# Cross-attention output and first gate tile by row blocks, with the gate's features split straight from PSUM

## The chip, the cores and the metric

One Trainium2 chip, one core. The metric is the device time of one execution in microseconds, lower is better; a kernel's time is the median of its runs.

## The reference

Two transformer blocks on 256 rows of width 2048, all in float32. The change lies in the second block, between the output projection of its cross attention and the gate of its feed-forward part:

```python
y = memory_cross_attention(h, mem_n, w_xq, w_xkv, w_xo)   # its last step: (256 x 512) @ w_xo (512 x 2048)
x = x + rms_norm_2(y, ln_x_post)                          # norm over each row's 2048 values
h = rms_norm_2(x, ln_ffn_pre)
y = (silu(h @ w_gate) * (h @ w_up)) @ w_down              # D_FF 5632
x = x + rms_norm_2(y, ln_ffn_post)
```

## The kernel before

**Products.** A weight matrix streams in as chunks of 512 rows by 512 columns (1 MB); half a chunk, 256 rows, is a *half*. The Scalar engine rounds a half into `whi` (`hi`, a 128x1024 cast, the helper's line 596) and the Vector engine puts the rest, raw minus `whi`, into `wlo` (`lo`, line 1415). Features stand transposed in `xhi` and `xlo` (128 features x 256 rows, 16 blocks `kb`), split in the same way. `half(q, ...)` on TensorE makes 12 matmuls of 512 columns: for two blocks of features and both row blocks b (rows 0 to 127 and 128 to 255), xhi by whi, xhi by wlo, xlo by whi (lines 2454 to 2456). It waits for `lo_done`, and its last matmul raises `pe_half`. `whi` and `wlo` hold four halves, so `hi(q)` waits until half q-4 has been used. A tile of 512 output columns takes two PSUM banks, one for each row block; `free(t)` makes TensorE wait until the tile two back has been read (`evicted`).

**The stretch of the change.** The output projection xo has four tiles of two halves each (q = xo0 to xo7), and TensorE goes through them tile by tile. After each tile the Scalar engine takes the sums of squares of both row blocks (`post_squares`, line 642) and the Vector engine multiplies the tile by the norm's gain into `ybuf` (`post_gained`, line 1591). After the last tile `post_norm(1)` works out 1/rms (lines 1609 to 1612), and `post_rows` (line 1600) adds `ybuf` times 1/rms to the residual h, 512 columns of one row block at a time. Then `turn_group` transposes h on TensorE in quads: four 128x128 transposes of one row block, one PSUM bank each, two quads a group (line 2520). The Vector engine multiplies a quad by the gain into `stage_t` (`turned_rows`, line 1527), the Scalar engine rounds it into `xhi` (`hi_group`, line 596), and the Vector engine writes the rest to `xlo` (`lo_group`, line 1538).

**The order.** Each engine works through one list written out by hand, and the engines meet at semaphores; nothing is planned at run time. TensorE: xo0 to xo7; group 0; then the gate's halves f0 to f7 over both row blocks, with groups 1, 2 and 3 behind f0, f2 and f4. Half f0 waits for the split of group 0, f2 for group 1, f4 for group 2 and f6 for group 3. Half f8, the first of the up projection, comes next. On the Scalar engine `square_sums(6)` (two passes over h, line 705) and a square root stand between the last `hi_group` and `hi` of f8; the Vector engine's `row_scale(6)` (lines 1505 and 1507) belongs to it. The DMA queue (SyncE) loads a chunk when `lo` of the chunk four back is done.

Of the kernel before, what the change touches and what calls it, by code (L numbers as in the profile page):

```python
# [3217 lines left out]
```

## Time and profile before

| | |
|---|---|
| median of 3 runs | 2511.58 us (2508.11 to 2513.05) |
| profiled execution | 2507.73 us, its span 2505.9 us |
| TensorE busy | 2474.0 us, 99% of the span |
| Vector engine busy | 1552.3 us, 62% |
| Scalar engine busy | 1238.7 us, 49% |
| mean granted TensorE clock | 0.997 |

Times in rows are microseconds from the start of the span unless marked ns. In the profile DVE is the Vector engine, ACT the Scalar engine, PE TensorE's matmuls and PEld its weight loads. A matmul's duration overlaps the next one's, so the pitch of the starts tells what it costs. The profiled execution is 1.83 us longer than its span and 3.85 us under the median.

### The profile page before, as it was taken

To read this page: it belongs to the slowest core of one execution; us is meant where nothing else is said; L and a number is where in the kernel's file an instruction comes from. 1 tells how busy PE (TensorE), PEld (TensorE's weight loads), DVE (VectorE), ACT (ScalarE), POOL (GpSimd) and SP (SyncE) were. 2 spreads that over 40 slices of the span, in tenths; PEclk is the share of its full clock that TensorE was granted. 3 is DMA by queue.
4 is the path that set the end of the run, shared out by engine and by line. 5 is a ranking of instruction groups with operands and counts; after the bars stand their busy time and mean duration, and the time that the engine had idled before them with its cause. 6 is when DMAs were issued, how large, how long until landed. Compare 5 with 4: busy or idle time off the path is not lost.

```text
span 2505.9 us, 31485 instructions
## 1 busy us (share of the span) xinstructions
PE 2474.0 (99%) x12033; PEld 2157.0 (86%) x12033; DVE 1552.3 (62%) x1941; ACT 1238.7 (49%) x1622; POOL 70.2 (3%) x57
## 2 busy tenths in 40 slices
PE   9999999999999999999999999999899999999998
PEld 8888888888888888888888778888788888888887
DVE  7576475655565655676555666766755555555557
ACT  7475554544444545445443445565554444444444
POOL 1022120000000000000000000000000000000000
PEclk9999999999999999999999999999999999999999
DMA  9655656656566565656654446675466666666664
GB/s 356 187 160 164 207 191 195 196 186 207 195 201 201 192 210 185 210 191 224 213 168 135 154 140 196 230 245 185 134 215 199 200 198 198 198 200 200 200 201 135
DMA packets 244712, 488.77 MB, mean 195 GB/s; under 512 B 11984, under 2 KB 13296, under 8 KB 243856
## 3 DMA queue, kind: packets, MB, share of 16 engines
q1 hardware_dynamic: 240592, 470.35, 58.0%
q0 software_dynamic: 3312, 13.92, 1.5%
q10 hardware_dynamic: 720, 3.29, 0.4%
q8 instruction: 60, 0.98, 0.2%
q14 instruction: 28, 0.23, 0.0%
HBM read 485.43 MB, written 2.10 MB: 195 GB/s over the span
## 4 chain that ended last, share of the span: by engine, by line
PE 95%; DVE 3%; ACT 2%; issue 1%; DMA 0%; DVEq 0%; ACTq 0%; SPq 0%
PE ps_a L2454 24%; PE ps_a L2456 24%; PE ps_a L2455 24%; PE ps_b L2454 5%; PE ps_b L2455 5%; PE ps_b L2456 5%; PE ps_b L2797 1%; DVE wlo L1415 1%; PE ps_b L2520 1%; PE ps_b L2585 0%; PE ps_b L2871 0%; ACT whi L596 0%; PE ps_b L2861 0%; ACT prob L1087 0%; PE ps_b L2886 0%
## 5 line engine op out<-in xcount | busy, mean ns | idle before, releaser
L1415 DVE TENSOR_TENSOR wlo<-raw,whi 128x1024 fp32r<-128x1024 f32 x872 | 1069.4, 1236 | 681.8 <-ACT whi L596 680.0
L596 ACT CAST whi<-raw 128x1024 fp32r<-128x1024 f32 x880 | 911.1, 1045 | 965.8 <-PE ps_a L2456 743.0
L2454 PE MATMUL ps_a<-whi,xhi 128*128 128x512 f32 x1888 | 725.5, 384 | 8.9 <-DVE wlo L1415 5.9
L2455 PE MATMUL ps_a<-wlo,xhi 128*128 128x512 f32 x1888 | 717.0, 380 | 0.0
L2456 PE MATMUL ps_a<-whi,xlo 128*128 128x512 f32 x1888 | 716.9, 380 | 0.0
L2454 PEld LDWEIGHTS ps_a<-whi,xhi 128*128 128x128 f32 x1888 | 357.8, 190 | 65.3 <-issue 11.0
L2456 PEld LDWEIGHTS ps_a<-whi,xlo 128*128 128x128 f32 x1888 | 357.7, 189 | 50.8
L2455 PEld LDWEIGHTS ps_a<-wlo,xhi 128*128 128x128 f32 x1888 | 357.9, 190 | 48.6
L2454 PE MATMUL ps_a<-whi,x2hi 128*128 128x512 f32 x640 | 244.8, 383 | 1.1 <-DVE wlo L1415 1.1
L2456 PE MATMUL ps_a<-whi,x2lo 128*128 128x512 f32 x640 | 242.7, 379 | 0.0
L2455 PE MATMUL ps_a<-wlo,x2hi 128*128 128x512 f32 x640 | 242.7, 379 | 0.0
L2454 PEld LDWEIGHTS ps_a<-whi,x2hi 128*128 128x128 f32 x640 | 121.1, 189 | 18.5 <-DVE wlo L1415 1.1
L2456 PEld LDWEIGHTS ps_a<-whi,x2lo 128*128 128x128 f32 x640 | 121.1, 189 | 17.1
L2455 PEld LDWEIGHTS ps_a<-wlo,x2hi 128*128 128x128 f32 x640 | 121.1, 189 | 16.4
L2454 PE MATMUL ps_b<-whi,uhi 128*128 128x512 f32 x320 | 121.4, 379 | 0.0
L2455 PE MATMUL ps_b<-wlo,uhi 128*128 128x512 f32 x320 | 121.3, 379 | 0.0
L2456 PE MATMUL ps_b<-whi,ulo 128*128 128x512 f32 x320 | 121.3, 379 | 0.0
L2454 PE MATMUL ps_a<-whi,muhi 128*128 128x512 f32 x272 | 103.4, 380 | 0.0
L2455 PE MATMUL ps_a<-wlo,muhi 128*128 128x512 f32 x272 | 103.1, 379 | 0.0
L2456 PE MATMUL ps_a<-whi,mulo 128*128 128x512 f32 x272 | 103.1, 379 | 0.0
L2455 PE MATMUL ps_b<-wlo,muhi 128*128 128x512 f32 x240 | 91.0, 379 | 0.0
L2456 PE MATMUL ps_b<-whi,mulo 128*128 128x512 f32 x240 | 91.0, 379 | 0.0
(406 smaller groups left out, 2217.3 us busy)
## 6 DMA issues: line engine op xcount, KB each, us to landing
raw<-in_w_in SPq DMA_DIRECT2D x108, 1024.0 KB, 5.6
raw<-in_w_up SPq DMA_DIRECT2D x108, 1024.0 KB, 5.4
raw<-in_w_down SPq DMA_DIRECT2D x108, 1024.0 KB, 5.0
raw<-in_w_gate SPq DMA_DIRECT2D x44, 1024.0 KB, 5.1
raw<-in_w_out SPq DMA_DIRECT2D x16, 1024.0 KB, 5.1
raw<-in_w_mix_out SPq DMA_DIRECT2D x16, 1024.0 KB, 6.3
raw<-in_w_br_attn SPq DMA_DIRECT2D x8, 1024.0 KB, 5.1
raw<-in_w_br_pool SPq DMA_DIRECT2D x8, 1024.0 KB, 5.0
```

Source lines behind the costliest of these rows:

```text
L596: return nc.scalar.copy(o, i)
L1415: return V.tensor_tensor(wlo[:, q % 4], raw[:, c % SLOTS, 2 * j:2 * j + 2], whi[:, q % 4].bitcast(F32), ALU.subtract).then_inc(lo_done, 1)
L2454: mm(o, x0, m0, start=first and j == 0, stop=False)
L2455: mm(o, x0, m1, start=False, stop=False)
L2456: ins = mm(o, x1, m0, start=False, stop=last and j == len(kbs) - 1)
L2520: ins = nc.tensor.transpose(o[:, m * P:(m + 1) * P], src[:, b, (kb + m) * P:(kb + m + 1) * P], ident)
L2797: ins = nc.tensor.transpose(ps[:, (b * 4 + j) * P:(b * 4 + j + 1) * P], src[:, b, j * P:(j + 1) * P], ident)
```

## The change

The semaphores `last_half` and `last_added`, used at the end of the kernel, are renamed `row_tile` and `row_taken` and counted on from what the new stretch adds; two counts of `post_std` and `post_var` at the end go up by one. The rest of the change is this:

- Tiles 2 and 3 of xo run by row blocks (`half_rows`, six matmuls): both tiles for b = 0, then both for b = 1. Only the b = 1 pass raises `pe_half`. Tiles 0 and 1 stay as they were.
- Squares, gain and norm of tiles 2 and 3 are taken per row block; each row block has its own norm and root.
- f0 to f3 run for b = 0, then for b = 1; f4 to f7 over both.
- Transposes come one quad at a time in the order `ROW_QUADS` (row block, column tile), eight turns instead of four groups.
- `turned_rows` and `stage_t` go: `row_hi` (Scalar) and `row_lo` (Vector) read the quad in PSUM, four instructions of 128x128 each with the gain as their per-partition scale.

```diff
...
+ROW_QUADS = ((0, 0), (0, 1), (1, 0), (1, 1), (0, 2), (1, 2), (0, 3), (1, 3))
+def row_quad(k):
+    b, j = ROW_QUADS[k]
+    bank_ = bank(4 + (QUADS["n6"][0] + k + 2) % 4)
+    return [(4 * j + m, slice(b * P, (b + 1) * P), bank_[:, m * P:(m + 1) * P]) for m in range(4)]
...
-    rest_xo = linear("xo", 0, 4, lambda t, tile, q: post_squares(tile, q), kchunks=1, opened=2, late=2)
-    c0, q0, _ = seg["ffn"]
-    for k in range(2):
-        hi(q0 + k, chunk=c0 + k // 2)
-    rest_xo()
-    post_norm(1)
-    for j in range(4):
-        if j == 0:
-            act.wait_ge(pe_half, q_end("xo"))
-        hi_group("n6", j, xhi)
-        if j < 3:
-            for k in range(2 * j + 2, 2 * j + 4):
-                hi(q0 + k, chunk=c0 + k // 2)
+    some("xo", 2, 4)
+    _, qx_, tx = seg["xo"]
+    post_squares(tx, qx_ + 2)
+    some("xo", 4, 8)
+    post_squares(tx + 1, qx_ + 4)
+    def row_squares_of(b, t):
+        if b:
+            act.wait_ge(pe_half, qx_ + 2 * t + 2)
+        else:
+            act.wait_ge(row_tile, t - 1)
+        act.wait_ge(post_sq, 8 + 4 + 2 * b + t - 2)
+        nc.scalar.activation(junk2[:, b * NT:(b + 1) * NT], bank(2 * (t % 2) + b), ACT.Square,
+                             accum_out=s_pp[:, 4 * b + t:4 * b + t + 1]).then_inc(post_sq, 1)
+    def row_root(b):
+        act.wait_ge(post_var, 2 + b)
+        nc.scalar.activation(s_pstd[:, b:b + 1], s_pvar[:, b:b + 1], ACT.Sqrt).then_inc(post_std, 1)
+    def row_hi(k):
+        act.wait_ge(t_ps, QUADS["n6"][0] + k + 1)
+        if k == 0:
+            act.wait_ge(pe_half, qx_ + 4)
+        for kb, r, ps in row_quad(k):
+            ins = nc.scalar.activation(xhi[:, kb, r], ps, ACT.Copy, scale=gain_t[:, G_FFN + kb:G_FFN + kb + 1])
+        ins.then_inc(t_hi, 1)
+    row_squares_of(0, 2)
+    row_squares_of(0, 3)
+    row_root(0)
+    some("ffn", 0, 1)
+    row_hi(0)
+    some("ffn", 1, 2)
+    row_hi(1)
+    row_squares_of(1, 2)
+    some("ffn", 2, 3)
+    row_squares_of(1, 3)
+    row_root(1)
+    some("ffn", 3, 4)
+    row_hi(2)
+    row_hi(3)
+    for k in range(4, 8):
+        some("ffn", k, k + 1)
+        row_hi(k)
     square_sums(6)
     act.wait_ge(post_done, 16)
...
     xo_gained = post_gained(1)
-    linear("xo", 0, 4, lambda t, tile: xo_gained(t, tile) if t < 3 else None, kchunks=1, opened=2, late=2)
-    c0, q0, t0 = seg["ffn"]
-    ffn_gain = gain_t[:, G_FFN:G_FFN + 16]
-    for k in range(2):
-        lo(q0 + k, chunk=c0 + k // 2)
-    post_norm(1)
-    post_group(0)
-    for j in range(4):
-        turned_rows("n6", j, ffn_gain)
-        if j == 1:
-            xo_gained(3, t0 - 1)
-        lo_group("n6", j, xhi, xlo)
-        if j < 3:
-            post_group(j + 1)
-            for k in range(2 * j + 2, 2 * j + 4):
-                lo(q0 + k, chunk=c0 + k // 2)
+    _, qx_, tx = seg["xo"]
+    def row_gained(b, t):
+        dve.wait_ge(post_sq, 8 + 4 + 2 * b + t - 1)
+        return V.tensor_tensor(streams(ybuf[:, b, t * NT:(t + 1) * NT]), columns(2 * (t % 2) + b),
+                               streams(post_gain[:, t * NT:(t + 1) * NT]), ALU.mult)
+    def row_norm(b):
+        dve.wait_ge(post_sq, 8 + 4 + 2 * b + 2)
+        link(V.reduce_sum(s_psq[:, b:b + 1], s_pp[:, 4 * b:4 * b + 4], axis=AX))
+        V.tensor_scalar(s_pvar[:, b:b + 1], s_psq[:, b:b + 1], 1.0 / D, EPS, ALU.mult, ALU.add).then_inc(post_var, 1)
+    def row_norm_end(b):
+        dve.wait_ge(post_std, 2 + b)
+        link(V.reciprocal(s_prstd[:, b:b + 1], s_pstd[:, b:b + 1]))
+    def row_residual(k):
+        b, t = ROW_QUADS[k]
+        post_rows([(t, b)])
+    def row_lo(k):
+        dve.wait_ge(t_hi, QUADS["n6"][0] + k + 1)
+        for kb, r, ps in row_quad(k):
+            ins = V.scalar_tensor_tensor(xlo[:, kb, r], ps, gain_t[:, G_FFN + kb:G_FFN + kb + 1], xhi[:, kb, r].bitcast(F32),
+                                         ALU.mult, ALU.subtract)
+        ins.then_inc(t_lo, 1)
+    some("xo", 2, 4)
+    dve.wait_ge(pe_half, qx_ + 2)
+    xo_gained(0, tx)
+    some("xo", 4, 8)
+    dve.wait_ge(pe_half, qx_ + 4)
+    xo_gained(1, tx + 1)
+    row_gained(0, 2).then_inc(row_taken, 1)
+    row_norm(0)
+    row_norm_end(0)
+    row_residual(0)
+    row_residual(1)
+    some("ffn", 0, 1)
+    row_lo(0)
+    some("ffn", 1, 2)
+    row_lo(1)
+    link(row_gained(0, 3))
+    some("ffn", 2, 3)
+    row_norm(1)
+    row_norm_end(1)
+    row_residual(2)
+    some("ffn", 3, 4)
+    row_gained(1, 2).then_inc(evicted, 1)
+    row_lo(2)
+    row_residual(3)
+    row_lo(3)
+    row_gained(1, 3).then_inc(evicted, 1)
+    dve.wait_ge(evicted, tx + 4)
+    for k in range(4, 8):
+        row_residual(k)
+        some("ffn", k, k + 1)
+        row_lo(k)
     row_scale(6)
     c0, q0, _ = seg["ffn"]
...
-    for t in range(1, 4):
-        tile("xo", t, 1)
-    def residual_added(j):
-        pe.wait_ge(post_done, 8 + 2 * (j + 1))
+    tile("xo", 1, 1)
+    def half_rows(q, b, o, k, first, last):
+        pe.wait_ge(lo_done, q + 1)
+        w0, w1_ = whi[:, q % 4], wlo[:, q % 4]
+        for j, kb in enumerate((2 * k, 2 * k + 1)):
+            x0, x1 = xhi[:, kb, b * P:(b + 1) * P], xlo[:, kb, b * P:(b + 1) * P]
+            m0, m1 = walked(w0[:, j]), walked(w1_[:, j])
+            mm(o, x0, m0, start=first and j == 0, stop=False)
+            mm(o, x0, m1, start=False, stop=False)
+            ins = mm(o, x1, m0, start=False, stop=last and j == 1)
+        if b:
+            ins.then_inc(pe_half, 1)
+        return ins
+    def row_turn(k):
+        n = QUADS["n6"][0] + k
+        b, j = ROW_QUADS[k]
+        pe.wait_ge(post_done, 8 + k + 1)
+        if k < 4:
+            pe.wait_ge(t_y, n - 3)
+        else:
+            pe.wait_ge(t_lo, n - 3)
+        for kb, _, ps in row_quad(k):
+            ins = nc.tensor.transpose(ps, h[:, b, kb * P:(kb + 1) * P], ident)
+        ins.then_inc(t_ps, 1)
+    free(t0 + 2)
+    for t in (2, 3):
+        if t == 3:
+            free(t0 + 3)
+        for k in range(2):
+            ins = half_rows(q0 + 2 * t + k, 0, bank(2 * (t % 2)), k, k == 0, k == 1)
+        ins.then_inc(row_tile, 1)
+    for t in (2, 3):
+        for k in range(2):
+            half_rows(q0 + 2 * t + k, 1, bank(2 * (t % 2) + 1), k, k == 0, k == 1)
+            if (t, k) in ((2, 1), (3, 0)):
+                row_turn(t - 2)
+    def split_rows(k):
+        pe.wait_ge(t_lo, QUADS["n6"][0] + k + 1)
     c0, q0, tile0 = seg["ffn"]
-    turn_group("n6", h, residual_added, 0)
-    for k in range(8):
-        if k == 0:
+    pe.wait_ge(row_taken, 1)
+    for b in range(SB):
+        if b:
             pe.wait_ge(evicted, tile0 - 1)
+        for k in range(4):
+            if k % 2 == 0:
+                split_rows(2 * b + k // 2)
+            half_rows(q0 + k, b, bank(b), k, k == 0, False)
+            if k % 2:
+                row_turn(2 + 2 * b + k // 2)
+    for k in range(4, 8):
         if k % 2 == 0:
-            pe.wait_ge(t_lo, QUADS["n6"][0] + k + 2)
-        half(q0 + k, (0, 1), (2 * k, 2 * k + 1), k == 0, k == 7)
-        if k in (0, 2, 4):
-            turn_group("n6", h, residual_added, k // 2 + 1)
+            split_rows(k + 1)
+        half(q0 + k, (0, 1), (2 * k, 2 * k + 1), False, k == 7)
+        if k < 6:
+            row_turn(k + 2)
     pe.wait_ge(evicted, tile0)
```

## Rows read from the trace of the kernel before

**Rows 1.** Busy time of each engine over the whole span, the page's first part.
```profile
PE 2474.0 (99%) x12033; PEld 2157.0 (86%) x12033; DVE 1552.3 (62%) x1941; ACT 1238.7 (49%) x1622; POOL 70.2 (3%) x57
```
**Rows 2.** TensorE's waits: for whom, us in total, times, longest.
```profile
PE ps_b L2520 <- DVE h L1600: 3.6, 1, 3.6
PE ps_a L2454 <- issue: 2.2, 1, 2.2
```
**Rows 3.** Timeline of TensorE from xo7 to f8: start, us, idle before.
```profile
1789.88 0.38 PE L2456 MATMUL ps_a<-whi,xlo 128*128 128x512 f32 x1
1793.90 1.77 PE L2520 MATMUL ps_b<-base,h 128*128 128x128 f32 x8 [3.64 <-DVE h L1600]
1797.88 0.77 PE L2454 MATMUL ps_a<-whi,xhi 128*128 128x512 f32 x1 [2.21 <-issue]
...
1802.07 1.04 PE L2520 MATMUL ps_b<-base,h 128*128 128x128 f32 x8
1802.86 0.46 PE L2454 MATMUL ps_a<-whi,xhi 128*128 128x512 f32 x1
1803.16 0.38 PE L2455 MATMUL ps_a<-wlo,xhi 128*128 128x512 f32 x1
...
1825.15 0.45 PE L2454 MATMUL ps_a<-whi,xhi 128*128 128x512 f32 x1 [0.90 <-DVE wlo L1415]
```
**Rows 4.** Timeline of the Scalar engine, the same stretch and what leads to it.
```profile
1779.93 0.60 ACT L642 ACTIVATE junk<-ps_a 128x512 f32<-128x512 f32 x1 [2.02 <-PE ps_a L2456]
1781.09 2.00 ACT L596 CAST whi<-raw 128x1024 fp32r<-128x1024 f32 x2
1790.30 0.60 ACT L642 ACTIVATE junk<-ps_a 128x512 f32<-128x512 f32 x1 [2.02 <-PE ps_a L2456]
1817.93 1.91 ACT L705 ACTIVATE junk<-h 128x2048 f32<-128x2048 f32 x1
```
**Rows 5.** Timeline of the Vector engine, the same stretch.
```profile
1780.76 1.29 DVE L1591 TENSOR_TENSOR ybuf<-ps_a,post_gain 128x512 f32<-128x512 f32 x2 [1.41 <-ACT junk L642]
1782.17 2.36 DVE L1415 TENSOR_TENSOR wlo<-raw,whi 128x1024 fp32r<-128x1024 f32 x2
1791.59 0.16 DVE L1609 TENSOR_REDUCE small<-small 128x2 f32<-128x8 f32 x1 [1.89 <-ACT junk L642]
1792.43 1.41 DVE L1600 SCALAR_TENSOR_TENSOR h<-ybuf,small,h 128x512 f32<-128x512 f32 x2
1802.71 1.29 DVE L1527 TENSOR_TENSOR stage_t<-ps_b,gains 128x512 f32<-128x512 f32 x2 [1.34 <-PE ps_b L2520]
```
**Rows 6.** The nearest small pieces, Scalar engine: four of 128x128 from PSUM with a per-partition scale.
```profile
136.29 1.14 ACT L900 ACTIVATE proj<-ps_a,small 128x128 f32<-128x128 f32 x4
137.30 1.06 ACT L596 CAST whi<-raw 128x1024 fp32r<-128x1024 f32 x1
```
**Rows 7.** The nearest small pieces, Vector engine; the last row groups 128x128 reads of PSUM.
```profile
344.91 1.66 DVE L1769 SCALAR_TENSOR_TENSOR olo_a<-ps_b,gains,ohi 128x256 fp32r<-128x256 f32 x4 [1.79 <-ACT ohi L991]
L1769 DVE SCALAR_TENSOR_TENSOR olo_a<-ps_b,gains,ohi 128x256 fp32r<-128x256 f32 x8 | 3.3, 477 | 1.8 <-ACT ohi L991 1.8
L2061 DVE CUSTOM_DVE_ANT_0 prob<-ps_b,bias 128x128 f32<-128x128 f32 x32 | 9.1, 284 | 0.0
```
**Rows 8.** Stretches: us, PE busy, PEld, DVE, ACT, POOL, PEclk, DMA share, GB/s.
```profile
1757.70:1762.30 4.60, 2.33 (x19) 1.95 (x18) 4.40 (x11) 3.50 (x6) 0.00 (x0) 1.00 0.00 0
1793.90:1797.88 3.98, 1.77 (x9) 1.40 (x9) 2.77 (x5) 2.06 (x3) 0.00 (x0) 0.53 0.07 27
1797.88:1801.00 3.12, 3.12 (x8) 2.50 (x9) 3.12 (x4) 1.07 (x2) 0.00 (x0) 0.50 0.00 0
1801.00:1825.15 24.15, 22.51 (x114) 18.90 (x113) 17.94 (x27) 14.27 (x18) 0.00 (x0) 1.00 0.48 158
```
**Rows 9.** Timeline of TensorE ahead of the 16 transposes of the attention weights.
```profile
1757.70 0.38 PE L2456 MATMUL ps_a<-whi,x2lo 128*128 128x512 f32 x1
1760.35 1.97 PE L3050 MATMUL ps_b<-base,pr 128*128 128x128 f32 x16 [2.27 <-DVE pr L2304]
```

More of the change, by code:

```diff
@@ L306, in hybrid_blocks_kernel @@
         u_row_done, u_tps, u_hi, u_lo, d_add = sem("u_row"), sem("u_tps"), sem("u_hi"), sem("u_lo"), sem("down_added")
-        last_half, last_add = sem("last_half"), sem("last_added")
+        row_tile, row_taken = sem("row_tile"), sem("row_taken")
         ns = {n: sem("nsa_" + n) for n in ("dup", "tk", "xpe", "zero", "t2", "t2s", "hid", "gelu", "hidt", "hidr", "kv", "kvs", "t1", "t1s",
@@ L1295, in _ @@
                     n = 4 * b + t
-                    act.wait_ge(last_add, n + 1)
+                    act.wait_ge(row_taken, 1 + n + 1)
                     if n > 1:
@@ L1300, in _ @@
                                          accum_out=s_pp[:, n:n + 1]).then_inc(post_sq, 1)
-                act.wait_ge(post_var, 3 + b)
+                act.wait_ge(post_var, 4 + b)
                 nc.scalar.activation(s_pstd[:, b:b + 1], s_pvar[:, b:b + 1], ACT.Sqrt).then_inc(post_std, 1)
@@ L2382, in last_sum @@
             def last_sum(b, t):
-                dve.wait_ge(last_half, 4 * b + t + 1)
+                dve.wait_ge(row_tile, 2 + 4 * b + t + 1)
                 d = streams(ybuf[:, b, t * NT:(t + 1) * NT])
-                V.tensor_tensor(d, d, columns((2, 3, 0, 1)[t] if b == 0 else 4 + t), ALU.add).then_inc(last_add, 1)
+                V.tensor_tensor(d, d, columns((2, 3, 0, 1)[t] if b == 0 else 4 + t), ALU.add).then_inc(row_taken, 1)
             def last_gain(b, t):
-                dve.wait_ge(last_add, 4 * b + t + 1)
+                dve.wait_ge(row_taken, 1 + 4 * b + t + 1)
                 c = slice(t * NT, (t + 1) * NT)
@@ L2398, in last_rows @@
                 V.tensor_scalar(s_pvar[:, b:b + 1], s_psq[:, b:b + 1], 1.0 / D, EPS, ALU.mult, ALU.add).then_inc(post_var, 1)
-                dve.wait_ge(post_std, 3 + b)
+                dve.wait_ge(post_std, 4 + b)
                 link(V.reciprocal(s_prstd[:, b:b + 1], s_pstd[:, b:b + 1]))
@@ L3089, in _ @@
                 half(q0 + k, (2 * (t0 % 2), 2 * (t0 % 2) + 1), (2 * k, 2 * k + 1), k == 0, k == 1)
-            for t in range(1, 4):
-                tile("xo", t, 1)
-            def residual_added(j):
-                pe.wait_ge(post_done, 8 + 2 * (j + 1))
-            assert seg["xo"][2] % 2 == 0
+            tile("xo", 1, 1)
[11 more added lines that the diff above has]
+                return ins
@@ new lines, in row_turn @@
+            def row_turn(k):
[9 more added lines that the diff above has]
+                ins.then_inc(t_ps, 1)
+            assert t0 % 2 == 0
@@ L3165, in _ @@
                             ins = mm(o, x1, m0, start=False, stop=kb == 3)
-                    ins.then_inc(last_half, 1)
+                    ins.then_inc(row_tile, 1)
 _INS = ["x", "mem", "w_in", "gla_a_w2", "fox_f_b", "w_mem_kv", "w_out", "w_up", "w_down", "mem_2", "ln_mix_post_2", "ln_x_post_2",
```

## The prediction

> **What bounds the kernel now.** The page's busy times come first: TensorE is busy for 2474.0 of 2505.9 us, the Vector engine for 62% [rows 1]. Only what fills a hole of TensorE, or opens one, moves the time. Its waits come next, and two of the longest single ones belong to the stretch of the change: 3.6 us for the residual h, and 2.2 us before the first gate matmul, marked "issue" [rows 2]. The timeline gives their place [rows 3]: the last matmul of xo starts at 1789.88 and the first of f0 at 1797.88, with eight transposes between. The squares of tile 1 start at 1779.93 and those of tile 3 at 1790.30 [rows 4], so two tiles (48 matmuls) take 10.37 us, 0.216 us each. So xo ends at 1790.10, f0 starts 7.78 us later, and tile 1 ended at 1779.74. In the hole the clock falls to the lower level: granted 0.53 from 1793.90 and 0.50 to 1801.00, then 1.00 [rows 8]. f0, twelve matmuls that should take 2.59 us, lasts from 1797.88 to 1802.07, 1.60 us too long.
>
> From 1779.74 to the start of f8 at 1825.15 [rows 3] pass 45.41 us. Tiles 2 and 3 and f0 to f7 are 144 matmuls, 31.07 us. The other 14.34 us are holes, slow clock and transposes: that is all the change can touch. Behind f8 the same loop goes on as before, so the change is worth what it does to the start of f8.
>
> **What stays, and the prices.** Matmuls, transposes (32), weights and their DMAs keep their number. A 512-column residual add costs 0.66 us behind another and 0.75 alone, a gain 0.60 and 0.69, `lo` 1.14 and 1.22 [rows 5], `hi` 0.95 and 1.05 [rows 4]; squares with their accumulator read take 0.58 (1779.93 to 1781.09 for two [rows 4]), 0.70 until readable. A norm takes 0.84 from its sum to the first residual add (1791.59 to 1792.43 [rows 5]). Four transposes take 0.40 (eight in 0.79 [rows 3]), the matmul behind a switch or a stall 0.08 more (pitch 0.30 at 1802.86 [rows 3]). A quad can be read 0.64 after its turn starts (1802.07 to 1802.71 [rows 3, 5]), 0.70 after a stall. Between engines I take 0.04 to 0.08.
>
> **The new split.** `row_hi` is four 128x128 reads of PSUM with a per-partition scale. The nearest row has just that form: four in 1.14, the next instruction 1.01 after the first [rows 6]. `row_lo` has no row. Four reads of PSUM of 256 columns in the same operation take 1.66 at 0.477 each, a pitch of 0.39 [rows 7]; 512 columns have a pitch of 0.66 [rows 5]; that is 0.27 for 256 columns, so 0.26 for a piece of 128 and 1.13 for four. From the start of a turn to the matmul that uses the quad it is then 0.70 + 0.04 + 1.13 + 0.04 + 1.13 + 0.08 = 3.1 us. Bounds: no less than one 512-column instruction each (0.60 on the Scalar engine, like the read of 1779.93 [rows 4], 0.69 on the Vector engine, like that of 1802.71 [rows 5]), and no more than four whole durations without overlap, 4 x 0.38 and 4 x 0.34 (0.477 less 0.13; 0.284 is the shortest 128-column read of PSUM [rows 7]).
>
> The Trainium skill ("VectorE: DVE Perf Modes", section on the errata of SBUF-source operations) says that an instruction pays a fixed cost whatever its size, and advises pieces of 512 elements or more, which speaks against four pieces of 128. By its figures for reads of PSUM a piece would take an estimated 0.25 us on the Scalar engine and 0.26 on the Vector engine; the sum by it would be the same, and the row of the Scalar engine (0.253) agrees.
>
> **The walk along the three queues**, in times of the old span:
> 1. Tile 2 for b = 0 ends at 1782.33. Tile 3 needs the banks of tile 1, whose gain used to run from 1780.76 to 1782.05 [rows 5], long before tile 3. Now `hi` of xo7 stands ahead of the squares (1779.90 to 1780.95, it waits for the end of tile 1), and `lo` of xo7 ahead of the gain (to 1782.13). The two gains end at 1783.42 and TensorE has stood for 1.17.
> 2. Tile 3 for b = 0 ends at 1786.18, its squares at 1787.08, the residual add of quad 0 at 1788.76. Meanwhile tile 2 for b = 1 runs until 1788.77. Turn 0 waits 0.07. Turn 1 and tile 3 for b = 1 run to 1792.45, and the split of quad 0 is there at 1791.82. So f0 starts at once: the hole of 7.78 and the 1.60 of slow clock are gone.
> 3. f0 and f1 for b = 0 end at 1795.04. Turn 2 needs the norm of b = 1. xo7 is done at 1792.45, but its squares stand behind `hi` f1, `row_hi` 1, the squares of tile 2 and `hi` f2 and start at 1794.01; the norm's sum stands behind `lo` f2 (to 1795.78). The residual ends at 1797.42: turn 2 at 1797.50, 2.46 lost.
> 4. Turn 3 needs a residual that stands behind `lo` f3, a gain and `row_lo` 2, which waits for `row_hi` 2: 1801.22, 0.59 lost. Turn 4 stands behind `row_lo` 3 and a gain: 1805.67, 1.32 lost. Turn 5 behind `row_lo` 4: 1809.39, 0.59 lost.
> 5. f4 wants the quad that turn 5, just ahead of it, brings: a bare split, 1812.45, 2.52 lost. Before, a half of 2.59 stood between a group and its use.
> 6. Turn 7 waits for the residual behind `row_lo` 6 (0.59), and f6 for turn 7 (2.52): 1821.85.
> 7. The squares of h start behind `row_hi` 7 at 1820.48. From their start to f8 it was 7.22 (1817.93 to 1825.15 [rows 3, 4]), now 7.19: f8 at 1827.67, 0.56 behind f7.
>
> The waits: 1.17 + 0.07 + 2.46 + 0.59 + 1.32 + 0.59 + 2.52 + 0.59 + 2.52 + 0.56 = 12.39. With 31.07 for matmuls, 8 turns of 0.48 (3.84) and 0.63 for ten restarts it is 47.93, against 45.41: **2.5 us slower**. The same walk along the old lists puts f8 at 1825.11; it stands at 1825.15.
>
> The loads are hidden: the chunk of f6 and f7 is asked for when `lo` of xo7 ends (1782.13; before, at 1784.53 [rows 5]) and is wanted at 1811; that of f8 behind `lo` f1 at 1792.9, wanted at 1825, and the queues were busy for 0.48 of this stretch or less [rows 8]. GpSimd has nothing here. The later end-of-kernel edits are names and counts: nothing.
>
> The profiled execution becomes 2507.73 + 2.5 = 2510.2. The median shown is 3.85 above that execution; 2511.58 + 2.5 = **2514.1 us**. With the cheap bounds for the pieces the walk gives 2.9 less than before, with the dear ones 7.0 more.
>
> **Rivals.** *The clock falls again.* Before, it fell after 3.64 us with no work [rows 3, 8]; it stayed at 1.00 through 2.27 us of nothing followed by sixteen transposes [rows 8, 9]. In the new order TensorE has only four transposes from 1808.80 to 1812.45 and from 1818.20 to 1821.85, and the longest empty piece is 2.5 us, nearer the row that kept it. If it falls ahead of f4 or f6, that half costs 1.60 more, as f0 did (f6 has the 0.56 ahead of f8 as cover): +4.1 with f4 alone, +5.2 with both, +6.8 if f2 behind turn 2 falls too. The point from which it decides is an empty piece of more than 2.3 and less than 3.6 us; with two or more the kernel is over 0.2% slower.
>
> *Pieces do not overlap on the Vector engine.* Then a `row_lo` takes 1.37 and the walk gives +4.2; with both engines so, +7.0. Against it: four pieces take 1.66, not 4 x 0.477 [rows 7].
> The Trainium skill ("VectorE: DVE Perf Modes", "The DRAIN you can't avoid") says that the next operation does not start before the pipeline has emptied. Read so, it would be this rival; the row of four pieces speaks against that reading.
>
> *Pieces are cheap*: as little as one wide instruction. f4 and f6 then wait 1.6 instead of 2.5, the other waits shrink too, and the time is up to 2.9 less.
>
> *The waits of steps 3, 5 and 6 do not come* and the removed hole is a gain: 2.5 - 2.46 - 2 x 2.52 = -5.0. For it: the hole is real and its filling certain. Against it: no size of a piece within the bounds gives it, and the order of TensorE's list puts f4 right behind turn 5.
>
> **Chances.** As walked (-0.5 to +4.5): 0.60. Cheap pieces: 0.08. Clock: 0.15, of which 0.09 for two falls or more. No overlap on the Vector engine 0.06, on both 0.05. The gain: 0.06. About 0.2%, 5.0 us, is what a measurement of this kernel can tell from no change. Faster by more than that: 0.06. Slower by more: 0.09 + 0.05 and 0.08 for the upper ends of the others and the scatter of the runs (4.9 us over three), 0.22. The rest, 0.72, is within. The range goes from -2.9 (cheap pieces) to +7.9 (dear pieces or three falls, with some scatter): 2508.7 to 2519.5.
>
> **What would show it.** Right: no hole of 7.8 us behind xo, clock at 1.00 there; a wait of 1.2 before tile 3 for the gain in `ybuf`; one of about 2.5 for h before turn 2; two of about 2.5 for `xlo` before f4 and f6; a quad's four pieces in about 1.1 us on each engine; f8 about 2.5 later after tile 1. Wrong: `xlo` waits under 1.5 (pieces cheap), a granted clock under 1 behind a turn (the clock), or f8 earlier than before.

## The result: 4.1 us slower, and where they are in the profile after

The changed kernel takes 2514.95 us in the median of 22 runs (2513.1 to 2516.81), the kernel before 2510.82 (22 runs, 2508.11 to 2513.05): the ratio is 1.0017 [1.0011, 1.0022], 2.8 to 5.5 us more. 2514.1 was predicted. The difference itself was predicted as +2.5, from a base of 2511.58, the median of three runs, which lies 0.76 above that of 22. So the time is close, in part by luck of the base, and the difference was 1.6 us short. Those 1.6 us are what there is to explain.

The profiled execution of the changed kernel takes 2515.64 us, its span is 2513.2: 7.91 more than the one before. Measured by the starts of TensorE's matmuls, 2.19 of them stand ahead of the change (tile 1 of xo ends at 1781.93 instead of 1779.74, in code that both kernels share), 0.61 outside the span, nothing behind f8 (from there to the end 680.72 and 680.75 us), and 5.14 in the stretch from the end of tile 1 to f8: 50.55 us instead of 45.41.

Most of the 2.19 us ahead of the stretch has one place. The sixteen transposes of the attention weights, which kept the full clock in the profile before [rows 8, 9], ran at the lower level here, behind a wait of the same length:

```profile
1760.88 3.63 PE L3136 MATMUL ps_b<-base,pr 128*128 128x128 f32 x16 [2.28 <-DVE pr L2344]
1764.17 0.56 PE L2540 MATMUL ps_a<-whi,x2hi 128*128 128x512 f32 x1
```

Before, the matmul behind them started at 1762.07:

```profile
1762.07 0.46 PE L2454 MATMUL ps_a<-whi,x2hi 128*128 128x512 f32 x1
```

They took 3.29 us instead of 1.72, which is 1.57 of the 2.19. The experiments come back to this place.

TensorE's waits in this stretch, in the view of waits (for whom, us in total, times, longest), answering [rows 2]:

```profile
PE ps_b L3202 <- DVE h L1640: 4.8, 5, 2.3
PE ps_a L2540 <- DVE xlo L2384: 4.8, 2, 2.4
PE ps_a L3185 <- DVE ybuf L1631: 1.1, 1, 1.1
```

The hole of [rows 3] is gone, and with it "issue". In its place stand eight waits, five of them for the residual h ahead of a turn, two for the split of one quad, one for the banks of tile 3. The timeline of TensorE tells where (start, us, instruction, idle before), and what the two longest do to the clock:

```profile
1785.74 0.48 PE L3185 MATMUL ps_a<-whi,xhi 128*128 128x512 f32 x1 [1.06 <-DVE ybuf L1631]
...
1799.52 0.66 PE L3202 MATMUL ps_b<-base,h 128*128 128x128 f32 x4 [2.27 <-DVE h L1640]
...
1811.38 0.66 PE L3202 MATMUL ps_b<-base,h 128*128 128x128 f32 x4 [0.46 <-DVE h L1640]
...
1814.42 0.48 PE L2540 MATMUL ps_a<-whi,xhi 128*128 128x512 f32 x1 [2.40 <-DVE xlo L2384]
...
1815.63 0.63 PE L2542 MATMUL ps_a<-whi,xlo 128*128 128x512 f32 x1
1816.06 0.63 PE L2540 MATMUL ps_a<-whi,xhi 128*128 128x512 f32 x1
...
1825.51 0.53 PE L2540 MATMUL ps_a<-whi,xhi 128*128 128x512 f32 x1 [2.40 <-DVE xlo L2384]
```

A turn is the four transposes of one quad. Turn 5 starts at 1811.38, f4 at 1814.42, turn 6 at 1818.62: f4 lasts 4.20 us. Inside it the pitch of the matmuls (from one start to the next) goes from 0.22 to 0.43 (1815.63 to 1816.06). The same stretches by windows (us, PE busy, PEld, DVE, ACT, POOL, PEclk, DMA share, GB/s), answering [rows 8]:

```profile
1811.38:1814.42 3.04, 0.65 (x4) 0.41 (x4) 2.25 (x6) 2.08 (x5) 0.00 (x0) 1.00 0.23 43
1814.42:1818.62 4.20, 4.20 (x13) 3.31 (x14) 1.74 (x2) 0.00 (x0) 0.00 (x0) 0.64 0.58 218
1825.51:1829.24 3.73, 3.73 (x9) 2.99 (x10) 0.34 (x2) 3.23 (x6) 0.00 (x0) 0.54 0.66 254
```

The clock is up in the hole and at its lower level (1.2 GHz) for most of f4 and of f6: granted 0.64 and 0.54.

The new split, which had no row before, on the Scalar and on the Vector engine:

```profile
1800.21 1.14 ACT L1261 ACTIVATE xhi<-ps_b,gains 128x128 fp32r<-128x128 f32 x4 [0.80 <-PE ps_b L3202]
1801.39 1.12 DVE L2384 SCALAR_TENSOR_TENSOR xlo<-ps_b,gains,xhi 128x128 fp32r<-128x128 f32 x4
1802.43 0.74 DVE L1640 SCALAR_TENSOR_TENSOR h<-ybuf,small,h 128x512 f32<-128x512 f32 x1
```

Busy times over the span, against [rows 1]: TensorE has the same 12033 matmuls, and its 5.7 us more are for the most part records stretched by the lower clock, which the two profiles have at different places.

```profile
PE 2479.7 (99%) x12033; PEld 2159.8 (86%) x12033; DVE 1551.3 (62%) x1960; ACT 1243.1 (49%) x1647; POOL 70.3 (3%) x57
```

### The profile page after: what moved, and what is told of

Its sections match the earlier page's. It is cut to its first block, busy times and chain, and to the rows that moved or that the text cites. A ratio compares the mean times of both kernels' runs of the same rounds, so it can differ in the third digit from the quotient of the medians.

```text
span 2513.2 us, 31528 instructions
## 1 busy us (share of the span) xinstructions
PE 2479.7 (99%) x12033; PEld 2159.8 (86%) x12033; DVE 1551.3 (62%) x1960; ACT 1243.1 (49%) x1647; POOL 70.3 (3%) x57
## 3 DMA queue, kind: packets, MB, share of 16 engines
q10 hardware_dynamic: 720, 3.29, 0.4%
## 4 chain that ended last, share of the span: by engine, by line
PE 95%; DVE 2%; ACT 2%; issue 1%; DVEq 0%; ACTq 0%
PE ps_a L2540 24%; PE ps_a L2541 24%; PE ps_a L2542 24%; PE ps_b L2541 5%; PE ps_b L2542 5%; PE ps_b L2540 5%; PE ps_b L2883 1%; PE ps_b L2957 1%; PE ps_b L2671 0%; DVE wlo L1455 0%; PE ps_b L2606 0%; ACT whi L604 0%; DVE xlo L2384 0%; PE ps_b L2947 0%; ACT prob L1095 0%
## 5 line engine op out<-in xcount | busy, mean ns | idle before, releaser
L2540 PE MATMUL ps_a<-whi,xhi 128*128 128x512 f32 x1856 | 713.9, 385 | 8.5 <-DVE xlo L2384 4.8
L2541 PE MATMUL ps_a<-wlo,xhi 128*128 128x512 f32 x1856 | 705.9, 380 | 0.0
L2542 PE MATMUL ps_a<-whi,xlo 128*128 128x512 f32 x1856 | 705.7, 380 | 0.0
L2540 PEld LDWEIGHTS ps_a<-whi,xhi 128*128 128x128 f32 x1856 | 352.2, 190 | 63.4 <-issue 6.9
L2542 PEld LDWEIGHTS ps_a<-whi,xlo 128*128 128x128 f32 x1856 | 352.3, 190 | 50.3
L2541 PEld LDWEIGHTS ps_a<-wlo,xhi 128*128 128x128 f32 x1856 | 352.3, 190 | 48.1
L2540 PE MATMUL ps_b<-whi,muhi 128*128 128x512 f32 x240 | 91.0, 379 | 0.0
```

The lines of the kernel that those rows point to most:

```text
L2540: mm(o, x0, m0, start=first and j == 0, stop=False)
L2541: mm(o, x0, m1, start=False, stop=False)
L2542: ins = mm(o, x1, m0, start=False, stop=last and j == len(kbs) - 1)
```

## The experiments

The measure is the stretch from the end of tile 1 (the start of tile 2's first matmul) to the start of f8, since both kernels are alike on either side. Last column: the ratio to the kernel before.

| kernel | stretch, us | clock falls in it at | ratio to before |
|---|---|---|---|
| before | 45.41 | group 0, f0 | 1 |
| changed | 50.55 | f4, f6 | 1.0017 [1.0011, 1.0022] |
| changed, again | 48.70 | turn 2 | one run |
| changed, once more | 49.91 | f6 | one run |
| 10 matmuls ahead of f4, f6 | 47.67 | none | 1.0008 [0.9999, 1.0017] |
| 3 matmuls ahead of f4, f6 | 47.67 | none | 1.0006 [0.9996, 1.0016] |
| residuals ahead | 47.22 | f4, f6 | 1.0007 [0.9998, 1.0017] |
| turns ahead | 45.69 | none | 0.9999 [0.9990, 1.0008] |
| turns and residuals ahead | 40.58 | none | 0.9975 [0.9965, 0.9985] |
| all three lists reordered | 36.50 | none | 0.9961 [0.9947, 0.9974] |
| split from PSUM, old order | 47.62 | group 0, f0 | 1.0003 [0.9994, 1.0012] |
| wide split, new order | 52.43 | turn 2, f6 | 1.0022 [1.0013, 1.0031] |
| before, hole filled | 43.52 | none | 0.9988 [0.9979, 0.9997] |

The difference of each stretch to 45.41, divided by 2511, lies within its interval in every row. So one stretch of one profile tells the time to about 1.5 us.

All experiments on the new order but the wide split have the three lists written out line by line, the two repetitions too. This moves one wait of the Vector engine, for the end of its last gain, from ahead of the residual of turn 4 to ahead of that of turn 7, and turn 4 then waits 1.06 us in the repetitions instead of 1.19. So beside these runs 0.13 us of the changed kernel's 50.55 belong to that wait.

**Is it the clock?** The changed kernel with ten matmuls of no use, into a bank that nothing holds, ahead of f4 and of f6:

```diff
             row_turn(5)
+            for _ in range(10):
+                mm(bank(2), xhi[:, 0, 0:P], walked(whi[:, (q0 + 4) % 4, 0]), start=True, stop=True)
             split_rows(5)
```

> The changed kernel with ten extra 512-column matmuls into a free PSUM bank ahead of f4 and ten ahead of f6, in the holes where TensorE waits for xlo. Theory (the second half of the loss is the clock, which falls in these two holes): granted clock 1.00 through f4 and f6, which take 2.6 us instead of 4.2 and 4.4; the stretch from the end of xo's tile 1 to f8, 50.55 us in the changed kernel, becomes 47.5 to 48.2, the waits ahead of f4 and f6 stay 2.4 to the end of the split, and the kernel is about 2.5 us slower than before (ratio 1.0010). Rival (f4 and f6 are slow for another reason, their operands or banks): they still take over 4 us, the stretch stays at 50.5. Rival (fillers get in the way): the stretch grows by 0.2 or more for each hole.

Timeline of TensorE, and the window of f4:

```profile
1811.28 2.40 PE L3264 MATMUL ps_a<-whi,xhi 128*128 128x512 f32 x10
1813.92 0.48 PE L2561 MATMUL ps_a<-whi,xhi 128*128 128x512 f32 x1 [0.23 <-DVE xlo L2392]
1829.22 0.45 PE L2561 MATMUL ps_a<-whi,xhi 128*128 128x512 f32 x1 [0.46 <-DVE wlo L1463]
```
```profile
1813.92:1816.61 2.69, 2.69 (x12) 2.33 (x13) 1.74 (x2) 0.00 (x0) 0.00 (x0) 1.00 0.90 338
```

f4 takes 2.69 instead of 4.20 us with the data no earlier, and f8 now waits the 0.46 us of the walk. The stretch is 47.67, and 47.80 with the 0.13 us of the moved wait: the two falls cost 2.75 us, and the rest of the change, +2.39, is the walk's +2.5. In time the interval reaches just under 1, and from this alone one could not tell the kernel from the one before.

**How little filling is enough?** Three matmuls instead of ten:

> The changed kernel with 3 instead of 10 matmuls of no use ahead of f4 and of f6, directly behind the turn. Each shortens the stretch with no work from 2.40 to 1.75 us; with the turn and the 0.46 us ahead of it, the work in the same piece rises from 0.4 to 1.1 us. Theory (the clock falls where a turn is all the work between two stretches with no work, the longer of them about 2.4 us): the clock stays at 1.00 at both places, the waits ahead of f4 and f6 are 1.7 us, and the stretch from the end of tile 1 to f8 takes 47.5 to 48.0 us, as with ten, time 2511 to 2513.5 us. Rival (the little work does not count, the clock needs the whole hole filled): a fall at one place at least, a half of 4.2 us there, stretch 49 us or more.

```profile
1814.34 0.48 PE L2561 MATMUL ps_a<-whi,xhi 128*128 128x512 f32 x1 [1.74 <-DVE xlo L2392]
...
1823.73 0.48 PE L2561 MATMUL ps_a<-whi,xhi 128*128 128x512 f32 x1 [1.74 <-DVE xlo L2392]
```

Waits of 1.74 us are left, f4 and f6 run at full clock, and the stretch is the same 47.67. The theory's numbers came, but two places in one profile are few, given what follows.

**Does the same wait always bring the clock down?** The changed kernel's three lists in their own order, profiled twice more. The two repetitions are the same kernel, line for line:

> The changed kernel's three lists, unaltered, profiled once more. Whether the clock falls behind the same 2.4 us of waiting every time is not known from one profile: with the split made wide it fell at turn 2 and f6 and stayed at f4 behind 2.46 us. Theory (the pattern decides): both falls again, f4 and f6 at 4.2 to 4.4 us, stretch 50.5 us. Rival (at 2.4 us it is a matter of chance in each execution): one of the two halves, or turn 2's block, differs from the first profile: 2.7 us instead of 4.2 or the other way round, stretch 47.7 to 49.5 or over 51.

> The same once more. Theory (the pattern decides): f4 and f6 at 4.2 to 4.4 us, stretch 50.5 us. Rival (chance): at least one of the two halves differs from the first profile in this or the other repetition.

First repetition, TensorE's timeline: turn 2 and the matmuls behind it, then f4 and f6.

```profile
1797.48 0.99 PE L3223 MATMUL ps_b<-base,h 128*128 128x128 f32 x4 [2.28 <-DVE h L1648]
1798.13 0.78 PE L3206 MATMUL ps_a<-whi,xhi 128*128 128x512 f32 x1
...
1813.26 0.48 PE L2561 MATMUL ps_a<-whi,xhi 128*128 128x512 f32 x1 [2.40 <-DVE xlo L2392]
1813.58 0.38 PE L2562 MATMUL ps_a<-wlo,xhi 128*128 128x512 f32 x1
...
1822.66 0.48 PE L2561 MATMUL ps_a<-whi,xhi 128*128 128x512 f32 x1 [2.40 <-DVE xlo L2392]
1822.98 0.38 PE L2562 MATMUL ps_a<-wlo,xhi 128*128 128x512 f32 x1
```

Second repetition, the same places:

```profile
1798.97 0.65 PE L3223 MATMUL ps_b<-base,h 128*128 128x128 f32 x4 [2.28 <-DVE h L1648]
...
1813.76 0.48 PE L2561 MATMUL ps_a<-whi,xhi 128*128 128x512 f32 x1 [2.40 <-DVE xlo L2392]
1814.08 0.38 PE L2562 MATMUL ps_a<-wlo,xhi 128*128 128x512 f32 x1
...
1823.16 0.80 PE L2561 MATMUL ps_a<-whi,xhi 128*128 128x512 f32 x1 [2.40 <-DVE xlo L2392]
1823.75 0.63 PE L2562 MATMUL ps_a<-wlo,xhi 128*128 128x512 f32 x1
```

A 0.63 behind a wait is the lower level, a 0.38 the upper. The waits ahead of turn 2, f4 and f6 agree to 0.01 us and the falls do not: f4 and f6 in the first profile, turn 2 alone in the second, f6 alone in the third. My theory, that the pattern decides, is refuted. Over all runs with the new order, the clock fell behind the 2.27 to 2.28 us ahead of turn 2 in 1 profile of 8, and behind the 2.39 to 2.46 us ahead of f4 or f6 in 6 places of 10. Behind 3.64 or more it fell in 3 of 3. The three profiles of the changed kernel have a mean stretch of 49.72, which is +4.3, and the runs' own difference is +4.1.

The sixteen transposes of the attention weights say the same with more profiles. Their code and what stands ahead of it are alike in all thirteen profiles of this document, and the wait ahead of them is 2.26 to 2.28 us in each. The granted clock from 1756 to 1766 was 1.00 in four of the profiles (before, the first repetition, the split from PSUM in the old order, the wide split) and 0.83 in the other nine. So the row from which the prediction took that 2.27 us keeps the clock [rows 8, 9] is itself one draw, and one that came up in 4 profiles of 13.

The Trainium skill ("TensorE: Matmul & The Clock Gate", section "What's actually happening") describes the monitor behind the clock as running freely, not counted from the instructions; equal waits with unequal falls are what that would give. No run here shows the monitor itself.

**The Vector engine's order.** Residual adds go ahead of the splits, and the last gain goes ahead of the split of quad 3; nothing else is touched. In the lists res is `row_residual`, rlo `row_lo`, lo f a half's `lo`, g(b,t) a `row_gained`:

```diff
-res2 lo f3 g(1,2) rlo2 res3 rlo3 g(1,3) res4 lo f4 rlo4 res5 lo f5 rlo5 res6 lo f6 rlo6 res7 lo f7 rlo7
+res2 res3 lo f3 g(1,2) rlo2 res4 g(1,3) rlo3 res5 lo f4 rlo4 res6 lo f5 rlo5 res7 lo f6 rlo6 lo f7 rlo7
```

> The changed kernel with one list altered, the Vector engine's: each residual add of b = 1 and of the second half of the columns stands ahead of the split of the quad before it, not behind. Theory (the waits ahead of turns 3, 4, 5 and 7 are the Vector engine's order): these four waits (0.46, 1.19, 0.46, 0.46) are gone, those of 2.4 ahead of f4 and f6 stay, since f4 and f6 stand right behind their turns; the stretch from the end of tile 1 to f8 goes from 50.55 to 47.3 to 48.0 with the clock falling as before, to 44.5 to 45.0 if it no longer falls. Rival (the four-piece splits set the pace, each quad's chain of turn and split being longer than a half): the waits move to the splits and the stretch stays above 49.

All of TensorE's waits for h but one are gone in the view of waits, and the clock falls at f4 and f6:

```profile
PE ps_a L2561 <- DVE xlo L2392: 4.8, 2, 2.4
PE ps_b L3223 <- DVE h L1648: 2.3, 1, 2.3
```
```profile
1809.64:1814.02 4.38, 4.38 (x12) 3.51 (x13) 1.74 (x2) 0.00 (x0) 0.00 (x0) 0.61 0.67 231
```

The stretch is 47.22. At equal falls (f4 and f6) the changed kernel took 50.55, or 50.42 without the 0.13, so the edit gives 3.2 us: the four waits of 0.46 to 1.06 us ahead of turns 3, 4, 5 and 7, 2.44 in sum, and their restarts.

**TensorE's order.** The turns go one or two blocks of six matmuls earlier. f.k.b is a block of half k for row block b; T is a turn:

```diff
-f.2.0 f.3.0 T3 f.0.1 f.1.1 T4 f.2.1 f.3.1 T5 f4 T6 f5 T7 f6 f7
+f.2.0 T3 f.3.0 f.0.1 T4 f.1.1 f.2.1 T5 f.3.1 T6 f4 T7 f5 f6 f7
```

> The changed kernel with TensorE's list alone altered: turns 3 to 7 stand one to two blocks of six matmuls earlier (turn 3 behind f2 of b = 0, turn 4 behind f0 of b = 1, turn 5 behind f2 of b = 1, turn 6 behind f3 of b = 1, turn 7 behind f4), so that work of TensorE lies between a turn and the half that uses it; the lists of the Scalar and Vector engines stay. Theory (the waits of 2.4 us ahead of f4 and f6 are the bare split, because nothing stood between turn and use; the residual adds still set the turns): the waits for xlo ahead of f4 and f6 are gone, those for h grow: turn 2 2.4, turn 3 1.9, turn 4 1.2, turn 5 0.6, turn 6 1.9, turn 7 0.6, and 0.6 ahead of f8. In sum 2.6 us less waiting than the walk of the changed kernel: 45.4 us from the end of tile 1 to f8 if the clock stays up, where the changed kernel took 50.55 and would have taken 47.7 with its clock up; 47 to 48.5 if the clock falls behind one of the waits for h. Time 2510 to 2513 us. Rival (the Vector engine's whole list sets the pace and nothing is gained by TensorE's order): 47.5 or more with the clock up at 1.00.

```profile
PE ps_b L3223 <- DVE h L1648: 7.8, 6, 2.3
```

The 4.8 us for `xlo` are gone and 3.0 of them come back as waits for h: a turn asked for earlier waits longer for a residual that comes no sooner. None of its waits is over 2.27, and the clock stays at 1.00. 45.69 for 45.4 expected.

**Both.** The two edits together:

> The same list of TensorE, and the Vector engine's residual adds one row_lo ahead as well (both reorderings together). Alone the first is walked to save 2.6 us of waits and the second 0.7. Theory: together they save more than their sum, since each alone only moves the wait to the other: waits left are 2.4 ahead of turn 2, 1.4 ahead of f4 and 0.6 ahead of f8, the stretch from the end of tile 1 to f8 takes 39 to 40.5 us with the clock at 1.00, and the time is 2503.5 to 2506.5 us, about 0.25% under the kernel before. Rival (effects add up): 44.5 or more, time 2509 or more.

```profile
1808.75 0.48 PE L2561 MATMUL ps_a<-whi,xhi 128*128 128x512 f32 x1 [1.18 <-DVE xlo L2392]
...
1820.34 0.46 PE L2561 MATMUL ps_a<-whi,xhi 128*128 128x512 f32 x1 [0.45 <-DVE wlo L1463]
```

The stretch is 40.58, 0.1 above what was expected, and the time 2503.54 us (9 runs), 0.25% [0.15%, 0.35%] under the kernel before. The 0.7 us that this expectation gives to the residuals alone was a mistake of mine: it sets a stretch with two falls against one without. At equal clock the residuals alone give 3.2 us, the turns alone 2.0 (47.67 to 45.69), and both 7.1 (47.67 to 40.58), still 1.9 more than their sum. With the turns ahead a late residual shows at once as a wait; with the residuals ahead the bare splits at f4 and f6 are left. Each edit takes away what limits the other.

**Or do the small pieces cost the time?** First the new split alone, in the kernel before (its hi, lo and order of groups stay; the quads of a group are read from PSUM in pieces):

```diff
-                turned_rows("n6", j, ffn_gain)
...
-                lo_group("n6", j, xhi, xlo)
+                for k in range(2 * j, 2 * j + 2):
+                    dve.wait_ge(t_hi, QUADS["n6"][0] + k + 1)
+                    for kb, r, ps in psum_quad(k):
+                        ins = V.scalar_tensor_tensor(xlo[:, kb, r], ps, gain_t[:, G_FFN + kb:G_FFN + kb + 1], ...)
```

> The kernel before with one part of the change alone: xhi and xlo of the gate's features are split straight from PSUM in four pieces each, in the old order (tiles of xo whole, groups of two quads, f0 to f7 over both row blocks). Theory (the split from PSUM is neutral, the order by row blocks is what loses): the stretch from the end of tile 1 to f8, 45.41 us before, is 44.9 to 46.0, the ratio within 0.0004 of 1. Rival (the pieces are the loss): 47 us or more, ratio 1.0008 or more.

```profile
1793.91 1.94 PE L2535 MATMUL ps_b<-base,h 128*128 128x128 f32 x8 [3.64 <-DVE h L1610]
1798.53 0.76 PE L2467 MATMUL ps_a<-whi,xhi 128*128 128x512 f32 x1 [2.68 <-issue]
```
```profile
1793.91:1798.53 4.62, 1.94 (x9) 1.57 (x9) 2.26 (x9) 3.44 (x10) 0.00 (x0) 0.51 0.07 25
1798.53:1803.78 5.25, 5.25 (x12) 4.01 (x13) 4.68 (x6) 0.61 (x1) 0.00 (x0) 0.50 0.14 18
```

My theory missed here: the stretch is 47.62, 2.2 more than before. A group of two quads needs 4.62 us from turn to f0 instead of 3.98, and the clock comes back only behind f0, which takes 5.25 instead of 4.19. The time (2510.34, 11 runs) does not tell the two kernels apart. So with two quads to a group the pieces do cost: from the turn to f0 it is 0.64 us more, the split of a pair being longer in pieces than wide. Another 1.06 is the longer time of f0 at the lower clock, and after the repetitions above one profile does not show that this comes each time.

Then the other half: the new order with the wide split through `stage_t`.

```diff
-                for kb, r, ps in row_quad(k):
-                    ins = V.scalar_tensor_tensor(xlo[:, kb, r], ps, gain_t[...], xhi[:, kb, r].bitcast(F32), ALU.mult, ALU.subtract)
+                V.tensor_tensor(v, bank(4 + (n + 2) % 4)..., gain_t[...]..., ALU.mult).then_inc(t_y, 1)
+                dve.wait_ge(t_hi, n + 1)
+                V.tensor_tensor(xlo[...], v, xhi[...].bitcast(F32), ALU.subtract).then_inc(t_lo, 1)
```

> The changed kernel in its order, with the split as it was before: one 512-column gain into stage_t (Vector), one 512-column rounding (Scalar), one 512-column subtraction (Vector), in place of four pieces of 128x128 from PSUM on each engine. A wide split from turn to use takes about 0.7 + 0.69 + 0.05 + 0.6 + 0.05 + 0.75 + 0.1 = 2.9 us against 3.1 for the pieces, but the Vector engine gives 1.4 us of work to a quad instead of 1.13 and stands still while the Scalar engine rounds. Theory (the order costs the time, the pieces nothing): the waits ahead of f4 and f6 stay at 2 to 2.4 us, the others grow by up to 0.5 each, the stretch takes 50 to 52.5 us and the time is 2514 to 2517 us, the changed kernel's or a little more. Rival (the pieces of 128x128 cost the time): the stretch takes under 49 us and the time is under 2513 us.

```profile
1800.17 1.12 PE L3207 MATMUL ps_b<-base,h 128*128 128x128 f32 x4 [4.37 <-DVE h L1641]
...
1816.48 0.48 PE L2545 MATMUL ps_a<-whi,xhi 128*128 128x512 f32 x1 [2.46 <-DVE xlo L2390]
1816.80 0.38 PE L2546 MATMUL ps_a<-wlo,xhi 128*128 128x512 f32 x1
...
1825.71 0.79 PE L2545 MATMUL ps_a<-whi,xhi 128*128 128x512 f32 x1 [2.46 <-DVE xlo L2390]
1826.30 0.63 PE L2546 MATMUL ps_a<-wlo,xhi 128*128 128x512 f32 x1
```

52.43, and 2516.21 us in the median: the pieces are not what makes the new order slow. The wait ahead of f4 is the same with either split (2.46 and 2.40); the one ahead of turn 2 is not. It grows to 4.37, far more than the 0.5 I allowed, because the Vector engine stands while the Scalar engine rounds quads 0 and 1, and the norm of b = 1 is behind that.

**What did the clock cost the kernel before?** Its hole is filled, 17 matmuls ahead of group 0 and 9 behind it:

```diff
+            pe.wait_ge(evicted, tile0 - 1)
+            pe.wait_ge(lo_done, q0 + 1)
+            for _ in range(17):
+                mm(bank(0), whi[:, q0 % 4, 1, 0:P], walked(whi[:, q0 % 4, 0]), start=True, stop=True)
             turn_group("n6", h, residual_added, 0)
+            for _ in range(9):
...
```

> The kernel before with matmuls of no use in its hole: 17 of 512 columns ahead of the first group of transposes, which waits 3.64 us there, and 9 behind it, ahead of f0, which waits 2.21 us. No real work is added or moved. Theory (the clock fell in the hole and slowed the group and f0): the granted clock stays at 1.00, the group takes 0.79 instead of 1.77, f0 2.6 instead of 4.19, part of which f2's wait for its split takes back; the stretch from the end of tile 1 to f8 takes 43 to 44.3 us instead of 45.41, and the time is 1 to 2.4 us under the kernel before. Rival (f0 was slow for another reason, such as a weight half or its xlo coming late): f0 stays at about 4.2 us with the clock at 1.00, and the stretch at 45.4.

```profile
1794.51 1.09 PE L2520 MATMUL ps_b<-base,h 128*128 128x128 f32 x8
...
1798.03 0.45 PE L2454 MATMUL ps_a<-whi,xhi 128*128 128x512 f32 x1 [0.48 <-issue]
```
```profile
1798.03:1800.69 2.66, 2.66 (x12) 2.29 (x13) 2.66 (x4) 1.01 (x2) 0.00 (x0) 1.00 0.00 0
```

f0 takes 2.66 instead of 4.19 us at a clock of 1.00, the stretch 43.52, and the time is 2507.77, 0.9988 [0.9979, 0.9997] of before: matmuls of no use make the kernel 0.8 to 5.3 us faster, 1.89 of it seen in the stretch.

**The version that beats both.** The same row blocks and the same split, with all three lists reordered by the walk: turns 2 to 7 earlier (turns 0 and 1 one block later), residuals ahead, the squares and gains of tile 1 ahead of `hi` and `lo` of xo7, the squares for the norm of b = 1 ahead of `row_hi` 0 and 1, and the squares of h behind `hi` of f9 (f8 to f15 need no row scale).

```diff
-T: x.3.1.0 T1 x.3.1.1 f.0.0 f.1.0 T2 f.2.0 f.3.0 T3 f.0.1 f.1.1 T4 f.2.1 f.3.1 T5 f4 T6 f5 T7 f6 f7
+T: x.3.1.1 T1 f.0.0 T2 f.1.0 f.2.0 T3 f.3.0 T4 f.0.1 f.1.1 T5 f.2.1 f.3.1 T6 f4 T7 f5 f6 f7
-S: hi f0 rhi0 hi f1 rhi1 sq(1,2) hi f2 sq(1,3) root1 hi f3 rhi2 rhi3 ... hi f7 rhi7 squares of h
+S: hi f0 hi f1 sq(1,2) rhi0 sq(1,3) root1 rhi1 hi f2 hi f3 rhi2 rhi3 rhi4 hi f4 ... rhi7 hi f8 hi f9 squares of h
-V: lo f0 rlo0 lo f1 rlo1 g(0,3) lo f2 norm1 res2 lo f3 g(1,2) rlo2 res3 rlo3 ...
+V: g(0,3) res0 lo f0 res1 lo f1 rlo0 norm1 g(1,2) res2 rlo1 lo f2 res3 lo f3 res4 rlo2 res5 rlo3 res6 rlo4 ...
```

> The changed kernel with the three lists altered: turns one matmul block earlier, residual adds as soon as their norm is there, the gain of tile 1 ahead of the split of xo7, the squares of b = 1 ahead of the splits of b = 0, the squares of h behind the weights of f9 instead of ahead of f8. Theory (row blocks lose only by the order; every wait from 0.4 up has an instruction ahead of it in some list that could stand elsewhere): waits under 2 us in sum, no fall of the clock, the stretch from the end of tile 1 to f8 34.5 to 36.5 instead of 50.55, the kernel 9 to 11 us faster than before, ratio 0.9956 to 0.9964. Rival (Vector and Scalar engine have no room, so holes come back elsewhere): stretch over 40, ratio over 0.9980.

All of TensorE's waits in the stretch:

```profile
1793.73 0.45 PE L3220 MATMUL ps_a<-whi,xhi 128*128 128x512 f32 x1 [0.71 <-issue]
1797.65 0.45 PE L3220 MATMUL ps_a<-whi,xhi 128*128 128x512 f32 x1 [0.30 <-DVE wlo L1471]
```
```profile
1781.60:1818.10 36.50, 35.36 (x177) 30.14 (x176) 31.82 (x64) 27.82 (x62) 0.00 (x0) 1.00 0.53 171
```

2501.15 us (5 runs, 2498.11 to 2501.46), 0.39% [0.26%, 0.53%] under the kernel before and 13.8 us under the changed one. The stretch is at the upper end of what was expected; of the 36.50 us 1.01 are waits.

## Why the prediction was right, and where it was not

**The walk held.** Each wait that it named is in the profile, for the releaser that it named:

| place | walked | measured |
|---|---|---|
| tile 3, gain of tile 1 | 1.17 | 1.06 |
| turn 0 | 0.07 | 0 |
| turn 2, norm of b = 1 | 2.46 | 2.27 |
| turns 3, 4, 5, 7, for h | 0.59, 1.32, 0.59, 0.59 | 0.46, 1.19, 0.46, 0.46 |
| f4, f6, bare split | 2.52 each | 2.40 each |
| f8 | 0.56 | 0.46 with the clock up in f6, 0 behind a fall there |
| stretch with the clock up | 47.93 | 47.80 (47.67 and the 0.13 of the moved wait) |

The steady 0.1 too much of each is small beside the sum: +2.5 walked, +2.39 measured with the clock up.

**The new split** was priced at 1.13 us for each engine and took 1.14 and 1.12, the next instruction on the Vector engine starting 1.04 behind the first piece. Neither cheap pieces nor pieces without overlap came true. By the rule of "The DRAIN you can't avoid" read strictly (the Trainium skill, "VectorE: DVE Perf Modes"), four pieces would take the sum of their durations; a start of the next instruction at 1.04 speaks against that reading once more, and the section itself adds that an operation which is not held starts earlier. The rivals on the order (no waits, a gain) fell with the walk.

**The hole's removal** gave what the walk said: no wait behind xo, f0 at full clock.

**The step that failed is the clock's chance.** I argued from two rows, one that kept the clock (2.27 us of nothing and sixteen transposes [rows 8, 9]) and one that lost it (3.64 us [rows 3, 8]), that 2.5 us was "nearer the row that kept it", and gave 0.15. Every profile of the changed kernel has at least one fall, and the first has the two that the rival priced: +5.14 measured, +5.2 written for it. The price of a fall was right (f4 4.20 against 2.69: 1.51, written 1.60) and so was the place for f4 and f6. What was wrong is the belief that between two rows lies a point which decides. Neither row was a fixed point: the place of the one that kept its clock lost it in 9 profiles of 13. The clock falls behind one and the same wait and stays up behind it, and fell 6 times in 10 at 2.4 us, so the sum should have carried it as an expected cost: with the measured shares, 6/10 of two falls and 1/8 of one, at 1.0 to 2.2 us each, some 2 us. The walk's 2.39 and the mean cost of the falls in the three profiles, 2.0 (2.75, 1.03 and 2.24), make 4.4; the runs gave 4.1. I had also read that the new places have four transposes about them where the row that kept its clock had sixteen, and gave it no weight. Even that would have misled me: where sixteen stood, the clock fell more often (9 of 13) than where four did.

**The base.** 2511.58 was 0.76 us high. It hid a part of the error, and that was luck: with 2510.82 the forecast would have read 2513.3, 1.6 under the median and not 0.85. The single profiled execution was forecast as 2510.2 and took 2515.64: 2.6 of that miss lie in the stretch, 2.19 ahead of it and 0.61 outside the span.

**What stays open.** Why some places fall more often than others. The length of the wait alone does not say it: 2.26 to 2.28 us ahead of sixteen transposes fell in 9 profiles of 13, 2.27 to 2.28 ahead of turn 2, four transposes and then matmuls, in 1 of 8, both behind matmuls without a pause. f4 and f6, with four transposes ahead of the wait and matmuls behind it, stand between (6 of 10). This points to the transposes beside the wait, but no run alters their number and nothing else. That the falls are chance from one execution to the next rests on two profiles of one program, three with the moved wait, and on the thirteen of the sixteen transposes; no run shows where the chip takes its measure.

## What to carry to other kernels

Fill a hole by moving work, but look at what the order leaves directly between a producer's turn and its consumer: f4 behind turn 5 waited for a bare split, and one block of other work there took that wait away. When two engines are late in turn, moving one list alone earns less (2.0 or 3.2 us) than its share of both together (7.1): walk all lists at once. And a wait near the length at which the clock fell before is to be priced as a chance times the cost, not as "near the row that kept it": that row is one execution, and in another the same place may have lost its clock.

## What was not expected of the hardware

- The granted clock after equal waits differs between executions of one program: behind 2.40 us it was 1.00 in one and 0.50 to 0.64 in another. In the changed kernel's profiles TensorE worked at the lower level for 3.4 us (turn 2, second profile) up to 5.7 us (f6 in the third, from 1823.16 to 1828.87, granted 0.50), and with the split from PSUM in the old order it was down for over 9 us (1793.91 to 1803.78, granted 0.51 and 0.50).
- Three matmuls of no use (0.65 us) ahead of each of two waits went with no fall in the one profile taken, as ten did; by the repetitions, one profile does not show that three are enough.
- 26 matmuls of no use in a hole made a kernel 0.8 to 5.3 us faster: f0 behind them took 2.66 us at a clock of 1.00 instead of 4.19 at the lower level.
- Behind the same wait (2.26 to 2.28 us) in the same code, the sixteen transposes of the attention weights ran at the lower level in 9 profiles of 13.
- The start of the stretch varied from 1779.73 to 1781.97 us over profiles in which everything ahead of it is the same. It follows the falls ahead of it, at about 147, 1258, 1495 and 1761 us: the seven profiles with one of them start it at 1779.73 to 1780.34, the six with two or three at 1781.36 to 1781.97. Those 2.2 us of the scatter of single runs have nothing to do with the change.
